# A two-layer hybrid decoder step: start, token shift and feed-forward norm rearranged, and the experts' gate and up products turned round

## The reference, cut to what matters

```python
for l in range(DEPTH):                                   # 2
    h = rmsnorm(x, W['norm_mix'][l])
    proj = h @ W['w_in'][l]                              # 1024 -> 4352 columns
    ya, xr, xi = s5_branch(proj[..., :o_a], ...)
    yb, s_fin, sh = rwkv7_branch(proj[..., o_a:o_b], ...)
    m = sigmoid(proj[..., o_b:o_c]) * ya + sigmoid(proj[..., o_c:]) * yb
    x = x + m @ W['w_out'][l]
    h2 = rmsnorm(x, W['norm_ffn'][l])
    x = x + (swiglu(h2, w1, w3, w2) if l % 2 == 0 else moe_ffn(h2, ...))
y = rmsnorm(x, W['norm_final'])

def rmsnorm(x, g):  return x * rsqrt(mean(x * x) + 1e-6) * g
def swiglu(h, w1, w3, w2): return (silu(h @ w1) * (h @ w3)) @ w2
def rwkv7_branch(p, shift0, ...):                        # token shift, 1792 columns
    prev = concatenate([shift0[:, None], p[:, :-1]])
    z = p + (prev - p) * mu
    ...
def moe_ffn(h, w_router, w1, w3, w2):                    # 8 experts, 1024 -> 3584 -> 1024
    top_v, top_i = lax.top_k(h @ w_router, 2); gates = softmax(top_v)
    for e in range(8): out += combine[..., e] * swiglu(h, w1[e], w3[e], w2[e])
```

## Time and profile before

| | |
|---|---|
| median of 3 runs | 2256.25 us (2254.21 to 2258.53) |
| the profiled execution: its time | 2257.98 us |
| its span, first to last instruction | 2255.8 us |
| mean granted TensorE clock | 0.933 of 2.4 GHz |
| start to the experts' first product | 0 to 1231.7 us |
| experts | 1231.7 to about 2226 us |
| busy share of the span | PE 91%, DVE 70%, ACT 45%, POOL 16% |

### The profile page before, as it was taken

The page is one execution under the profiler, slowest core; times in us unless marked ns, Lnnn a source line. Parts: engine busy times, 40 slices in busy tenths (PEclk is TensorE's granted clock), DMA queues, the critical chain, the costliest instruction groups (busy, mean ns, idle before and its releaser), DMA issues.

```text
span 2255.8 us, 29759 instructions
## 1 busy us (share of the span) xinstructions
PE 2056.7 (91%) x11490; PEld 1690.4 (75%) x11490; DVE 1573.3 (70%) x1960; ACT 1012.1 (45%) x1184; POOL 359.5 (16%) x315
## 2 busy tenths in 40 slices
PE   3998789898999997788895999999999999999996
PEld 2775577778999775577774888888888888888884
DVE  3586766325544777766324889898988889898984
ACT  1012323104433111333103777777767677777773
POOL 0553600200000554501201010101010100100000
PEclk7997999598999998999695999999999999999998
DMA  6333000144443333000142999999999999999990
GB/s 241 112 114 112 3 1 1 59 166 180 169 168 131 112 131 113 3 1 1 40 167 81 365 377 355 354 362 359 357 364 357 360 366 353 366 360 352 364 361 36
DMA packets 71627, 466.71 MB, mean 207 GB/s; under 512 B 12453, under 2 KB 13349, under 8 KB 16325
## 3 DMA queue, kind: packets, MB, share of 16 engines
q1 hardware_dynamic: 62352, 449.11, 53.7%
q0 software_dynamic: 3184, 13.24, 1.5%
q10 hardware_dynamic: 5956, 2.50, 0.4%
HBM read 459.74 MB, written 5.08 MB: 206 GB/s over the span
## 4 chain that ended last, share of the span: by engine, by line
PE 79%; DVE 7%; issue 6%; POOL 4%; ACT 2%; ACTq 1%; DMA 0%; SPq 0%; DVEq 0%; POOLq 0%
PE bank L526 77%; PE bank L1105 1%; ACTq L1183 1%; POOL arena L376 1%; DVE arena L1660 1%; PE bank L673 1%; ACT arena L1168 1%; POOL arena L390 1%; DVE arena L1490 0%; POOL arena L397 0%; DVE ring L1791 0%; DVE ring L1815 0%; DVE ring L1803 0%; ACT ring L1168 0%; POOL arena L408 0%
## 5 line engine op out<-in xcount | busy, mean ns | idle before, releaser
L2065 DVE TENSOR_TENSOR w_lo<-ring,w_hi 128x2048 fp32r<-128x2048 f32 x336 | 768.9, 2293 | 109.1 <-ACT w_hi L1168 108.7
L1168 ACT ACTIVATE w_hi<-ring 128x2048 fp32r<-128x2048 f32 x336 | 643.5, 1916 | 183.2 <-PE bank L526 183.2
L526 PE MATMUL bank<-arena,ring 128*128 128x280 f32 (+1 forms) x1920 | 460.6, 408 | 48.1 <-DVE arena L1490 23.0
L526 PEld LDWEIGHTS bank<-arena,ring 128*128 128x128 f32 (+1 forms) x1920 | 354.8, 190 | 143.4 <-issue 39.1
L1168 ACT ACTIVATE arena<-bank 128x256 f32<-128x256 f32 (+4 forms) x300 | 117.7, 396 | 592.2 <-PE bank L526 576.5
L526 PE MATMUL bank<-w_hi,he_hi 128*128 128x512 f32 x896 | 365.4, 408 | 4.9 <-DVE w_lo L2065 4.9
L526 PE MATMUL bank<-w_hi,he_lo 128*128 128x512 f32 x896 | 353.8, 395 | 0.0
L526 PE MATMUL bank<-w_lo,he_hi 128*128 128x512 f32 x896 | 353.4, 394 | 0.0
L526 PEld LDWEIGHTS bank<-w_hi,he_lo 128*128 128x128 f32 x896 | 169.0, 189 | 39.3
L526 PEld LDWEIGHTS bank<-w_hi,he_hi 128*128 128x128 f32 x896 | 169.1, 189 | 37.2 <-issue 5.3
L526 PEld LDWEIGHTS bank<-w_lo,he_hi 128*128 128x128 f32 x896 | 169.8, 190 | 32.4
(11 more groups left out here) (261 smaller groups left out, 2634.9 us busy)
## 6 DMA issues: line engine op xcount, KB each, us to landing
ring<-wstream_dram SPq DMA_DIRECT2D x427, 1024.0 KB, 6.8
s<-s_dram POOLq DMA_DIRECT2D x2, 1024.0 KB, 14.7
o_rw_dram<-arena POOLq DMA_DIRECT2D x2, 1024.0 KB, 5.1
x<-x_dram SPq DMA_DIRECT2D x1, 1120.0 KB, 5.0
y_dram<-arena POOLq DMA_DIRECT2D x1, 1120.0 KB, 4.4
arena<-s_b_dram POOLq DMA_DIRECT2D x2, 512.0 KB, 7.5
arena<-s_c_dram POOLq DMA_DIRECT2D x2, 512.0 KB, 9.4
arena<-lora_up_dram POOLq DMA_DIRECT2D x2, 512.0 KB, 11.4
```

Source lines behind the costliest of these rows:

```text
L526: return nc.tensor.matmul(out, lhsT, rhs, start=start, stop=stop, **k)
L1168: return nc.scalar.activation(out, in_, func, **k)
L2065: v.tensor_tensor(w_lo[n % SPLIT], slot(n), w_hi[n % SPLIT].bitcast(F32), ALU.subtract)\
```

## The change

It has two independent halves. In the first half, four things move. SP loads lam and tv first, then four transfers, slot 0, x0 and the constants, and only then slots 1 to 6; ACT issues none of them. DVE does `discretise` and `rotation_points(0)` before the norm, the rest of the discretisation behind it. The token shift is split: ACT writes z = (1 - mu) p beside p as it empties PSUM, and DVE adds mu times the previous token in 14 operations, spread behind the scans of pairs 2, 4, 6 and 8. In the dense feed-forward the high and low parts are made of x times the gain, not yet divided by the root mean square; the division is two more DVE operations a tile behind the products, and the norm's own sum is done on PE behind the first tile. With it h_lo moves to another place of the arena, and layer 1's small weights (s5_b, s5_c, lora_up) are loaded only when the dense part is done (x_ready 2 instead of 1); s0 is loaded behind the fourth rotation table.

In the second half, CAP becomes 96, the slots of a step become one of gate and one of up weights, and in `up` the weights are the stationary operand, 128 columns of them at a time. The tokens move: high and low part side by side (192 columns) over the high weights, the high part alone (96 columns) over the low weights. The result lies with hidden columns on the partitions, which is what `down` needs, so `turn` goes. ACT copies one half of the sums out of PSUM, DVE adds the other, ACT takes the silu, POOL multiplies (`act_out`) and makes the low part (`act_low`), ACT the high part. `down` keeps its form, with 96 stationary columns instead of 128.

```diff
-CAP = 128
+CAP = 96
...
+            for t, n in ((lam, "lam"), (tv, "tv")):
+                sp.dma_start(t[:], a[n]).then_inc(S["lam_in"], 16)
             for t, n in FIRST:
                 sp.dma_start(t[:], a[n]).then_inc(S["first_in"], 16)
-
-            for s in range(RING):
+            sp.dma_start(ring[:, 0, :], a["wstream"][0]).then_inc(slot_in[0], 16)
+            sp.dma_start(x0[:], a["x0"]).then_inc(S["x0_in"], 16)
+            for t, n in CONSTS[1:]:
+                sp.dma_start(t[:], a[n]).then_inc(S["consts"], 16)
+            for s in range(1, RING):
                 sp.dma_start(ring[:, s, :], a["wstream"][s]).then_inc(slot_in[s], 16)
...
                 if l:
-                    pool.wait_ge(S["x_ready"], 2 * l - 1)
+                    pool.wait_ge(S["x_ready"], 2 * l)
...
+            def act_out(p, t):
+                pool.wait_ge(S["eup_part"], up_part(p, t, "silu"))
+                nc.gpsimd.tensor_tensor(act_e[:, t % 2], sil_e[:, t % 2], sum_e[:, t % 2, 1], ALU.mult).then_inc(S["eup_act"], 1)
+
+            def act_low(p, t):
+                pool.wait_ge(S["et_hi"], p * N_ITER + (t + 1))
+                nc.gpsimd.tensor_tensor(at_lo[:, t % 2], act_e[:, t % 2], at_hi[:, t % 2].bitcast(F32), ALU.subtract)\
+                    .then_inc(S["et_lo"], 1)
...
-                norm(1 + 2 * l)
+                if l:
+                    norm(1 + 2 * l)
...
                             last = split_products(pools[2 * (n % 2) + c][:, 0:T], (w_h[:, c, k, :], w_l[:, c, k, :]),
                                                   (h_hi[:, k, :], h_lo[:, k, :]), k == 0, k == DC - 1)
...
                     last.then_inc(S["up_ps"], 1)
+                    if n == 0:
+                        norm(1)
...
                 if part == 0 and t >= 2:
-                    pe.wait_ge(S["eup_act"], p * N_ITER + (t - 1))
-                w_h, w_l = (w.rearrange("p (k m) -> p k m", k=DC // 2) for w in w_split(p, SLOT_OF[f"up{part}", t]))
-                for c in range(DC // 2):
-                    k = part * (DC // 2) + c
-                    last = split_products(pools[t % 2], (he_hi[e % 2][:, k, :], he_lo[e % 2][:, k, :]),
-                                          (w_h[:, c, :], w_l[:, c, :]), k == 0, k == DC - 1)
+                    pe.wait_ge(S["eup_sum"], p * N_ITER + (t - 1))
+                w_h, w_l = (w.rearrange("p (k m) -> p k m", k=DC) for w in w_split(p, SLOT_OF[f"up{part}", t]))
+                for b in range(2):
+                    o, q = up_bank(t, part)[:, b], slice(b * P, (b + 1) * P)
+                    for k in range(DC):
+                        if k < DC - 1:
+                            mm(o, w_h[:, k, q], he[e % 2][:, k], k == 0, False)
+                        last = mm(o[:, 1], w_l[:, k, q], he[e % 2][:, k, 0], False, False)
+                    last = mm(o, w_h[:, k, q], he[e % 2][:, k], False, True)
                 last.then_inc(S["slot_done"], 1)
-
-            def turn(p, t):
...
-                    if 1 <= t <= N_ITER:
-                        turn(p, t - 1)
...
-                    for t, n in CONSTS[1:]:
-                        ac.dma_start(t[:], a[n]).then_inc(S["consts"], 16)
                 ac.wait_ge(S["norm_ps"], i + 1)
...
+                    c = n - CA
+                    fn(z[:, c, :], src, ACT.Identity, scale=one_mu[:, l, c:c + 1])
+                    ins = fn(prow[:, c, 1:T + 1], src, ACT.Identity)
...
+                ac.wait_ge(S["bo_out"], 1)
+                ac.wait_ge(slot_in[FFN_AT % RING], 16 * (FFN_AT // RING + 1))
+                fn(fw_hi[0], slot(FFN_AT), ACT.Identity).then_inc(S["ffn_hi"], 1)
+                ac.wait_ge(S["rw_out"], 32)
+                c0 = PV["norm_ffn"][0]
+                for c in range(DC):
+                    ac.wait_ge(S["wo_out"], c + 1)
+                    fn(h_hi[:, c, :], x[:, c, :], ACT.Identity, scale=pv[:, 0, c0 + c:c0 + c + 1]).then_inc(S["split_hi"], 1)
                 norm(1)
...
+            def low_products(p, t):
+                ac.wait_ge(S["slot_done"], p * N_SLOTS + (SLOT_OF["up1", t] + 1))
+                fn(sum_e[:, t % 2], up_parts(t, 1), ACT.Identity).then_inc(S["eup_part"], 1)
...
-                tt(z[:, :, 0:TP], prow[:, :, 0:TP], prow[:, :, 1:TP + 1], ALU.subtract)
-                step(tt(z[:, :, TP:T], shift0[:, l], prow[:, :, TP + 1:T + 1], ALU.subtract))
-                for c in range(CR):
-                    ins = v.tensor_scalar(z[:, c, :], z[:, c, :], col(l, "mu", c), None, ALU.mult)
-                step(ins)
-                tt(z, z, prow[:, :, 1:T + 1], ALU.add).then_inc(S["z_ready"], 1)
+                for c in tiles:
+                    ins = v.scalar_tensor_tensor(out=z[:, c, 0:TP], in0=prow[:, c, 0:TP], scalar=col(l, "mu", c),
+                                                 in1=z[:, c, 0:TP], op0=ALU.mult, op1=ALU.add)
...
-                    if j == 8:
-                        shifted(l)
+                    if 2 <= j <= 8:
+                        shifted(l, *range(2 * j - 4, min(2 * j, CR)))
...
+                        v.tensor_tensor(up_s[:, m % 2, :], rstd[:, 1, :], pools[2 * (m % 2)][:, 0:T], ALU.mult)\
+                            .then_inc(S["up_scaled"], 1)
+                        step(v.tensor_tensor(act_f[:, m % 2, :], rstd[:, 1, :], pools[2 * (m % 2) + 1][:, 0:T], ALU.mult))
...
+            def sum_out(p, t):
+                dve.wait_ge(S["eup_part"], up_part(p, t, "low"))
+                v.tensor_tensor(sum_e[:, t % 2], sum_e[:, t % 2], up_parts(t, 0), ALU.add).then_inc(S["eup_sum"], 1)
```

More of the change, by code:

```diff
@@ L321, in tail_buffers @@
             return views
-        FIRST = [(x, "x"), (lam, "lam"), (ones, "ones"), (eps, "eps"), (pv, "pv"), (tv, "tv")]
+        FIRST = [(x, "x"), (ones, "ones"), (eps, "eps"), (pv, "pv")]
         CONSTS = [(x0, "x0"), (blk, "blk"), (ident, "ident"), (before, "before"), (iota, "iota"),
@@ new lines, in fetch @@
+            def fetch(p, e):
+                n = p * E + e
+                pool.wait_ge(S["mw_out"], n + 1)
+                tick(p)
+                if e or not isinstance(p, int):
+                    pool.wait_ge(S["ga_ps"], p * (2 * E) + 2 * e)
+                    tick(p)
+                else:
+                    pool.wait_ge(S["h_stored"], 32)
+                nc.gpsimd.tensor_copy(rows[0:CAP], slot_iw[0:CAP, e % 2, 0:1]).then_inc(S["rows_ready"], 1)
+                pool.wait_ge(S["rows_ready"], n + 1)
+                tick(p)
+                nc.gpsimd.indirect_dma_start(he_f[0:CAP], None, h_rows, bass.IndirectOffsetOnAxis(ap=rows[0:CAP, 0:1], axis=0),
+                                             bounds_check=T - 1).then_inc(S["he_in"], 16)
@@ new lines, in act_out @@
+            def act_out(p, t):
[5 more added lines that the diff above has]
+                    .then_inc(S["et_lo"], 1)
+            def one_pass(p):
+                choose(p, 0)
+                fetch(p, 0)
+                for t in range(1, N_ITER + 1):
+                    e, g = divmod(t, NG)
+                    act_out(p, t - 1)
+                    act_low(p, t - 1)
+                    if e < E - 1 and g == G_YOUT:
+                        choose(p, e + 1)
+                    if e < E - 1 and g == G_ROWS + 1:
+                        fetch(p, e + 1)
@@ L549, in norm @@
                     pe.wait_ge(S["norm_sq"], DC * i + c + 1)
-                    last = mm(pools[0][:, 0:T], ones[:], squares(i)[:, c, :], c == 0, c == DC - 1)
-                    if c == 0 and i in (1, 3):
+                    last = mm(pools[4 if i == 1 else 0][:, 0:T], ones[:], squares(i)[:, c, :], c == 0, c == DC - 1)
+                    if c == 0 and i == 3:
                         last.then_inc(S["weights_used"], 1)
@@ L1060, in rows_of @@
                 pe.wait_ge(S["selp_ready"], p * E + (e + 1))
+                if e >= 2:
+                    pe.wait_ge(S["em_out"], p * (E * DC) + DC * (e - 1))
+                if e == 0 and isinstance(p, int):
+                    pe.wait_ge(S["ht_out"], 6)
                 if e or not isinstance(p, int):
@@ L1114, in down @@
                 for j in range(2):
-                    q = slice(j * CAP, (j + 1) * CAP)
                     for hf in range(2):
-                        last = split_products(pools[acc(e) + hf], (at_hi[:, t % 2, q], at_lo[:, t % 2, q]),
+                        last = split_products(pools[acc(e) + hf][0:CAP], (at_hi[:, t % 2, j], at_lo[:, t % 2, j]),
                                               (w_h[:, j, hf * 512:(hf + 1) * 512], w_l[:, j, hf * 512:(hf + 1) * 512]),
@@ L1768, in mix, with scaled_low @@
                     tt(gate[:, n, :], gate[:, n, :], gate[:, DC + n, :], ALU.add).then_inc(S["bo_out"], 1)
+                def scaled_low(c):
+                    c0 = PV["norm_ffn"][0]
+                    dve.wait_ge(S["split_hi"], c + 1)
+                    stt(out=h_lo[:, c, :], in0=x[:, c, :], scalar=pv[:, 0, c0 + c:c0 + c + 1], in1=h_hi[:, c, :].bitcast(F32),
```

(9 more changed lines are left out.)

239 lines of the change are left out of this document (115 added, 124 removed).

## The result

The changed kernel takes 2354.53 us (median of 4 runs, 2353.23 to 2359.22), beside 2257.33 for the kernel before: ratio 1.0437, 95% interval 1.0417 to 1.0456. Forecast were 2365 us, range 2325 to 2430. The profiled execution took 2355.76 us, its span is 2354.0 us at a mean granted clock of 0.942.

What follows compares the result with a forecast made beforehand. PE was taken to set the pace, in the experts with the weight transfers close behind. 2257.98 - 25 - 18 - 6 + 0 + 158 = 2367 us for a profiled-like execution, so 2365 us at the median, range 2325 to 2430.

Steps and rivals of the forecast that it cites:

- Experts, +158: Experts' `up`: 64 products a step at 0.112 us each, set by weight loads; +158 us, bounds +130 and +237.
- The equality of fp32r and plain loads: Experts' `up`: assumption that an fp32r load costs as much as a plain one, recorded at 188 ns against 190.
- a granted clock other than 1.00: Experts: listed sign that the forecast is wrong, if the stage runs at such a clock.
- Start, -25: Kernel start: first projection near 17 us instead of 33.57, waits removed; -25 us, bounds -16 and -27.
- Token shift, -18: Both mixers: DVE's 15.2 us block spread out, later pairs start earlier; -9 us a layer, bounds -15 and -27 in all.
- Dense part, -6: Between mixer and dense part: first tile follows at once, PE idles 5 us behind it; -6 us, bounds -9 and 0.
- six plain products: Trace evidence for the load price: six plain f32 products with 2 moving columns take 0.81 us, 0.112 us apart.
- The first (the load hides): Experts: fp32r load costs under 0.090 us, transfers become the bound; -59 us there, 2150 us in all; chance 0.12.
- The second (narrow fp32r at the plain price, 0.55 us a pair): Experts' `up`: narrow products cost like plain f32, +11.85 us a step, 3535 us; chance 0.04 together with the third.
- the third: Experts: over 96 tokens for one expert forces a second pass, +1150, near 3515 us; chance 0.04 together with the second.
- The fourth (POOL late): Experts: POOL operations over 4 us each set the step, +0.5 us, 2420 us; counted within the forecast's 0.83.

Runs made afterwards that it cites:

- e2: Kernel before with only the second half of the change (96 slots, new `up`); 2419.45 us, ratio 1.0723 to the kernel before.
- e6: Changed kernel with the products over the low weights moving 192 columns instead of 96; 2333.33 us, ratio 1.0347 to the kernel before.
- e9: Changed kernel without the products over the low weights in gate and up, splits and transfers kept; 2168.76 us, ratio 0.9614 to the kernel before.
- e8: Changed kernel with the products over the low weights using 64 of each 128 stationary columns; 2252.66 us, ratio 0.9985 to the kernel before.
- e11: e1 with 96 token slots instead of 128 in the old form of the experts; 2181.74 us, ratio 0.9682 to the kernel before.
- e10: Changed kernel plus seven plain products of 512 moving columns ahead of the experts' first product; 2337.32 us, ratio 1.0374 to the kernel before.
- e1: Kernel before with only the first half of the change (start, token shift, dense part), old experts; 2189.72 us, ratio 0.9702 to the kernel before.
- e3: Kernel before with only the start changed: transfer order, discretisation and rotation points ahead of the norm; 2222.36 us, ratio 0.9839 to the kernel before.
- e4: Kernel before with only the token shift split and spread; 2227.76 us, ratio 0.9871 to the kernel before.
- e5: Kernel before with only layer 0's feed-forward norm put behind the products; 2255.24 us, ratio 0.9976 to the kernel before.
- e7: Changed kernel with the products over the low weights moving 2 columns instead of 96; 2724.35 us, ratio 1.2041 to the kernel before.

## Why the prediction was right

Direction, mechanism and size of the deciding term hold. That the total comes within 11 us is in part luck: the first half brought 19 us more than forecast (-68 for -49) and the second cost 4 to 8 us more (+162 in e2, +166 by spans), and in the second a term that nobody had put down, 16 us of low clock, was mostly cancelled by a step that grew less than forecast.

*Experts, +158.* By spans it was +166.4 (from the first product to the end). The price of a product, 0.112 us because of its load, is what the loads of after, e6 and e9 show, and e8 shows that it falls with the load's columns. The equality of fp32r and plain loads, which the forecast had to assume, held: 0.112 for both. The step grew by 1.33 us instead of 1.42, 112 x 0.09 = 10 us less, since gathering and combining are cheaper with 96 slots (e11 shows 0.07 of it in the old form); the forecast had taken 1 us for this in all. Not foreseen were the 21.4 us at the start of the stage. About 5 of them are three steps of longer `up` (3 x 1.65, that is 7.17 - 5.52), which the forecast's 112 steps contain; the other 16 are the clock. So 158 - 10 + 16 = 164 of the 166.4. Between the first product and the first `down` e6 has 17 us less by wider products, e10 19 by wider products ahead. By the forecast's own list this was a sign of being wrong ("a granted clock other than 1.00"); it holds for 41 of the stage's 1157 us and left the rest of the sum as it was.

*Start, -25.* -28 at its own place, 1 us beyond the bound -27: the projection began at 16.91 ("near 17") and did not wait for slot 1. A single execution does not tell this finely: in e1's trace, with the same start, the first S5 products come at 37.98, 24.5 us earlier than before. The rest of e3's -36 came later, 2.4 us of it in two blocks at another clock.

*Token shift, -18.* Mis-sized: -29 by e4's ratio, beyond the bound -27, and -30.6 by the table (-10.3 - 4.4 - 15.9). What was counted, up to pair 14, came out as forecast: -10.3 for -9 in layer 0, and about as much in layer 1 (products of pair 14 at 877.06 and 817.48, -59.6 behind the -50.1 of the dense part). Wrong was to let the gain end with the pairs: 4.4 us in layer 0 and 6.4 in layer 1 stand behind them. There, in layer 0, the first product of the low-rank part waits for DVE, before and after:

```profile
208.57 10.13 PE L526 MATMUL bank<-arena 64*128 64x280 f32 x24 [4.71 <-DVE arena L1601]
219.28 4.07 PE L526 MATMUL bank<-arena,blk 128*128 128x280 f32 x8 [0.59 <-ACT arena L1168]
```

```profile
168.53 10.12 PE L570 MATMUL bank<-arena 64*128 64x280 f32 x24 [2.99 <-DVE arena L1661]
179.24 2.12 PE L570 MATMUL bank<-arena,blk 128*128 128x280 f32 x8 [0.58 <-ACT arena L1212]
```

The wait is 1.7 us shorter, and the eight products behind it take 2.12 us instead of 4.07 because the clock is up again (1.00 from 179 to 182, 0.55 from 219 to 224 before). These 3.7 us are most of the 4.4 in the table.

*Dense part, -6.* -7.4 in the whole change, 6.3 in e5's trace; the wait of "about 5 us" is 4.85. Alone it is worth 1 to 5 us at the end (e5).

*Reading of the rows.* What the earlier trace rows and the forecast call six plain products are six records, so three products; the price of 0.112 is one of a record with its load, which is what an fp32r product has one of, and the sum stands.

*Rivals.* The first (the load hides) is out by the loads' distance, and would have been worth at most a third of its price (e9). The second (narrow fp32r at the plain price, 0.55 us a pair) is out by the 0.22 of after, the third by the single pass (448 products of w_hi with at_hi, as before). The fourth (POOL late) did not come: 2.4 us an operation, under its bound of 4, and nobody waits for at_lo.

## What to carry to other kernels

Before making the weights the stationary operand, count loads: a product costs the longer of its own moving columns and the next one's load, and with fp32r operands 128 stationary columns cost as much time as about 250 moving ones (0.112 us at 0.00044 a column). Below that, fewer columns moved is no gain, and here it was a loss: in e7, with 2 columns instead of 96 and as many loads, the granted clock was the lowest of all (0.80 to 0.81 over the whole kernel). When an edit removes a wait, follow the engine beyond the wait: here a third of the gain of the token shift (10.8 of 30.6 us) lay behind the pairs, in the next wait and in the clock.

## What the runs showed of the hardware

- The same instruction stream with *more* columns in every second product ran faster (192 instead of 96: 2333 for 2354 us) and with fewer far slower (2 instead of 96: 2724 us), at equal distances wherever the clock was equal. PE was busy in all three.
- Products of 192 and 96 columns, load-bound, ran on at the upper level where they found it (1.00 from 1210 to 2200 in after, and from 1163 on in e10) and at the lower one where they found that (0.50 from 1170 to 1204 in after, without a gap).
- A product's recorded start is no measure of its price when loads bound: 0.155 and 0.068 us in turn, with loads evenly 0.112 apart.
- In e8 a load of 64 fp32r columns is recorded at 138 ns, one of 96 at 161 and one of 128 at 188: 0.7 to 0.8 ns for each further column, as for plain ones.
- A load costs by the clock too: those of 128 columns stand 0.112 us apart at 1.00 and 0.213 at 0.50.
